# Gathered rows of a mixture-of-experts block, turned by VectorE in 32x32 squares instead of by TensorE

## The reference, cut to what matters

```python
def expert_block(args):                    # xb: 128 rows (tokens) of one expert
    xb, e = args
    gu = xb @ w_gate_up[e] + b_gate_up[e]  # 1024 -> 2048
    gate, up = gu[:, :D_EXPERT], gu[:, D_EXPERT:]
    gate = jnp.minimum(gate, SWIGLU_LIMIT)
    up = jnp.clip(up, -SWIGLU_LIMIT, SWIGLU_LIMIT)
    act = (up + 1) * (gate * jax.nn.sigmoid(SWIGLU_ALPHA * gate))
    return act @ w_down[e] + b_down[e]     # 1024 -> 1024
xs = hp[row_tok].reshape(n_blocks, MOE_BLOCK, D)      # rows gathered by expert
ys = lax.map(expert_block, (xs, block_e)).reshape(p_max, D)
```

## Time and profile before

| | |
|---|---|
| median of 3 runs | 1661.62 us (1660.86 to 1662.49) |
| span of the profiled execution (first to last instruction) | 1658.6 us |
| the profiled execution's own time beyond its span | not given; the median lies 3.0 us above the span |
| PE busy | 1623.4 us, 98% |
| DVE busy | 1349.3 us, 81% |
| ACT busy | 1096.4 us, 66% |
| POOL busy | 303.9 us, 18% |

### The profile page before, as it was taken

The page is one execution under the profiler, slowest core; times in us unless marked ns, Lnnn a source line. Parts: engine busy times, 40 slices in busy tenths (PEclk is TensorE's granted clock), DMA queues, the critical chain, the costliest instruction groups (busy, mean ns, idle before and its releaser), DMA issues.

```text
span 1658.6 us, 24749 instructions
## 1 busy us (share of the span) xinstructions
PE 1623.4 (98%) x8080; PEld 1342.5 (81%) x8080; DVE 1349.3 (81%) x1098; ACT 1096.4 (66%) x1002; POOL 303.9 (18%) x204
## 2 busy tenths in 40 slices
PE   8999999999989999999999999999999999999995
PEld 6797777788887888888888888888888888888884
DVE  6974555423668999999999999999999999999994
ACT  5433444322356777877877778878778878778873
POOL 0000000401006622412211112111112111122110
PEclk8999999999998999999999999999999999999998
DMA  8331222432449999999999999999999999999993
GB/s 249 107 102 51 77 77 77 130 102 87 162 174 352 335 368 390 385 387 371 366 384 385 387 374 370 377 388 387 385 368 365 387 386 385 387 371 362 390 386 87
DMA packets 115018, 483.42 MB, mean 291 GB/s; under 512 B 13371, under 2 KB 56599, under 8 KB 65687
## 3 DMA queue, kind: packets, MB, share of 16 engines
q1 hardware_dynamic: 103892, 454.43, 70.0%
q0 software_dynamic: 11088, 28.48, 8.0%
HBM read 469.51 MB, written 22.26 MB: 297 GB/s over the span
## 4 chain that ended last, share of the span: by engine, by line
PE 92%; DVE 3%; POOL 1%; issue 1%; ACT 1%; DMA 1%; SPq 0%; ACTq 0%; DVEq 0%; POOLq 0%
PE ps L621 29%; PE ps L623 28%; PE ps L622 28%; PE ps L849 2%; PE ps L843 2%; DVE work L1402 2%; POOL slot_records L1709 1%; PE ps L730 1%; PE ps L750 1%; PE ps L739 1%; PE ps L879 1%; PE ps L885 0%; DMA r<-in_x 0%; DVE r L1410 0%; ACT zT L976 0%
## 5 line engine op out<-in xcount | busy, mean ns | idle before, releaser
L1278 DVE TENSOR_TENSOR zT<-raw,zT 128x2048 fp32r<-128x2048 f32 x96 | 217.8, 2294 | 48.8 <-ACT zT L976 48.8
L1278 DVE TENSOR_TENSOR zT<-more_raw,zT 128x2048 fp32r<-128x2048 f32 x96 | 220.2, 2294 | 12.7 <-ACT zT L976 12.6
L1278 DVE TENSOR_TENSOR w_lo<-raw,w_hi 128x2048 fp32r<-128x2048 f32 x96 | 219.0, 2286 | 4.7 <-ACT w_hi L976 1.7
L976 ACT ACTIVATE w_hi<-raw 128x2048 fp32r<-128x2048 f32 x96 | 184.2, 1918 | 53.2 <-PE ps L623 53.2
L1278 DVE TENSOR_TENSOR w_lo<-more_raw,w_hi 128x2048 fp32r<-128x2048 f32 x96 | 217.7, 2294 | 1.3 <-ACT w_hi L976 0.4
L621 PE MATMUL ps<-zT,xT 128*128 128x512 f32 x512 | 203.0, 396 | 0.5 <-DVE zT L1278 0.5
L976 ACT ACTIVATE zT<-more_raw 128x2048 fp32r<-128x2048 f32 x96 | 183.5, 1912 | 27.0 <-PE ps L623 27.0
L621 PE MATMUL ps<-w_hi,xT 128*128 128x512 f32 x512 | 199.8, 390 | 1.5 <-DVE xT L1534 1.0
L623 PE MATMUL ps<-zT,xT 128*128 128x512 f32 x512 | 199.8, 390 | 0.0
L622 PE MATMUL ps<-zT,xT 128*128 128x512 f32 x512 | 199.7, 390 | 0.0
L623 PE MATMUL ps<-w_hi,xT 128*128 128x512 f32 x512 | 199.6, 390 | 0.0
(11 more groups left out here) (265 smaller groups left out, 3288.2 us busy)
## 6 DMA issues: line engine op xcount, KB each, us to landing
more_raw<-in_w_gate_up SPq DMA_DIRECT2D x129, 1024.0 KB, 7.7
raw<-in_w_gate_up SPq DMA_DIRECT2D x127, 1024.0 KB, 8.5
raw<-in_w_down SPq DMA_DIRECT2D x65, 1024.0 KB, 8.2
more_raw<-in_w_down SPq DMA_DIRECT2D x63, 1024.0 KB, 7.7
raw<-in_w_in SPq DMA_DIRECT2D x29, 1024.0 KB, 5.4
r<-in_x SPq DMA_DIRECT2D x8, 512.0 KB, 6.2
raw<-in_w_branch_conv SPq DMA_DIRECT2D x4, 1024.0 KB, 5.4
raw<-in_w_out SPq DMA_DIRECT2D x4, 1024.0 KB, 5.0
```

The lines of the kernel that those rows point to most:

```text
L976: nc.scalar.activation(expert_pair(0, c), chunk, ACT.Copy).then_inc(split_hi, 2)
L1278: nc.vector.tensor_tensor(expert_pair(1, c), chunk, expert_pair(0, c).bitcast(F32), ALU.subtract).then_inc(split_lo, 2)
```

## The change

The 128 rows of a block are gathered as four quarters for each token: four indirect DMAs of 128 pieces of 1 KB instead of one of 128 rows of 4 KB. The 32 partitions of group b receive quarter b of the features, so that squares of 32x32 are all that is left to turn. One VectorE instruction turns the whole 128x1024 block square by square into a plain SBUF buffer `rows_raw` (`turn_rows`, in DVE's order behind split 10). ACT makes `xTh` from that buffer in one instruction (`rows`), DVE makes `xTl` in one (`rest_of_rows`). PE's transposes of rows are gone except those of block 0, which go into `aTh` and `aTl` (the activations' buffers, free then). The quarter row numbers of blocks 1 and 2 need one more small matmul; those of later blocks come from four more reads of the records and one GpSimd operation ahead of the first scatter.

```diff
@@ PE
-    if j == 10:
-        next_rows(0, 0)
-next_rows(0, 1)
 with pe.Fori(1, nblk) as g:
-    pe.wait_ge(turned_read, tile(g, BEGIN) - 1)
+    pe.wait_ge(rows_lo, g)
...
     for k in range(KD):
         down(g, 16 + k, k)
-        if k == 3:
-            next_rows(g, 0)
-            next_rows(g, 1)
@@ PE, ahead of block 0
+pe.wait_ge(early_parts, 2)
+pe.matmul(ps[:, 1, 2 * P:2 * P + NQ * (EARLY - 1)], cst[:, C_SAME:C_SAME + P], by_part[:, :], start=True,
+          stop=True).then_inc(early_quarters, 1)
@@ ACT
+def rows(g, units, later):
+    if units is not None:
+        sc.wait_ge(used, units)
+    sc.wait_ge(rows_turned, later)
+    nc.scalar.activation(xTh, rows_raw.rearrange("p (k n) -> p k n", n=P), ACT.Copy).then_inc(rows_hi, 1)
...
-    turned(g, ROWS0, xTh[:, 0:4, :], bk_T)
-    turned(g, ROWS1, xTh[:, 4:8, :], bk_T + 1)
+    rows(g, unit_base(g) + 16, g + 1)
@@ DVE
+def turn_rows(g):
+    ve.wait_ge(xs_in, 16 + 16 * NQ * g)
+    if not isinstance(g, int) or g > 1:
+        ve.wait_ge(rows_lo, g - 1)
+    nc.vector.transpose(rows_raw.rearrange("p (k b j) -> p k b j", k=KD, b=NQ),
+                        quarters.rearrange("p b (i k) -> p k b i", k=KD)).then_inc(rows_turned, 1)
+def rest_of_rows(g):
+    ve.wait_ge(rows_hi, g)
+    nc.vector.tensor_tensor(xTl, rows_raw.rearrange("p (k n) -> p k n", n=P), xTh.bitcast(F32),
+                            ALU.subtract).then_inc(rows_lo, 1)
...
+    if c == 10:
+        turn_rows(g + 1)
     if c in (10, 11):
         gate_part(g, c - 10)
         up_part(g, c - 10)
-turned(g, ROWS0, xTh[:, 0:4, :], xTl[:, 0:4, :], bk_T)
-turned(g, ROWS1, xTh[:, 4:8, :], xTl[:, 4:8, :], bk_T + 1)
+rest_of_rows(g + 1)
@@ POOL
-def gather(col=0):
-    nc.gpsimd.indirect_dma_start(
-        out=xs, out_offset=None, in_=h2_dram,
+def gather_quarters(kept):
+    for part in range(NQ):
+        nc.gpsimd.indirect_dma_start(
+            out=quarters[:, part, :], out_offset=None, in_=h2_quarters,
...
+for part in range(NQ):
+    gp.dma_start(quarter_slots[PQ * part:PQ * part + PQ], slot_dram.rearrange(
+        "(b j c) i -> j b c i", b=NQ, j=PQ)).then_inc(slots_in, 16)
...
-gp.wait_ge(slots_in, 16)
+gp.wait_ge(slots_in, 16 * (1 + NQ))
+nc.gpsimd.tensor_scalar(quarter_rows.rearrange("p c b -> p b c"), quarter_slots[:, :, :, 0], float(NQ),
+                        cst[:, C_QUARTER:C_QUARTER + 1], ALU.mult, ALU.add).then_inc(quarter_rows_ok, 1)
+gp.wait_ge(quarter_rows_ok, 1)
```

More of the change, by code:

```diff
@@ L63 @@
 NREC = NB * TOPK
-C_END = C_REC + NREC
+NQ = 4
+C_PART = C_REC + NREC
+C_QUARTER = C_PART + NQ
+C_SAME = C_QUARTER + 1
+C_END = C_SAME + P
+QW = D // NQ
+PQ = P // NQ
 FILL = 11
@@ L401, in hybrid_block, with tile, hi_tile @@
         rows_free = sem("rows_free")
-        BEGIN, ACT0, ACT1, ROWS0, ROWS1 = range(5)
         FIRST_ROWS = 3
[L410 to L415, removed]
+        def tile(g, half):
+            return 2 * g + (2 + half)
+        def hi_tile(g, half):
+            return 2 * g + (1 + half)
         def unit_base(g):
@@ L859, in _, with gate_up @@
             nblk = pe.value_load(ublk[0:1, NCOL:NCOL + 1], min_val=NE, max_val=MAXBLK)
-            def gate_up(g, j, gate_bank=bk_A):
+            def gate_up(g, j, gate_bank=bk_A, hi=xTh, lo=xTl):
                 k, s = divmod(j, 2)
@@ L867, in gate_up @@
                     c = slice(512 * half, 512 * half + 512)
-                    last = three(ps[:, (gate_bank, bk_B)[s] + half, :], xTh[:, k, :], xTl[:, k, :], wh[:, c], wl[:, c],
+                    last = three(ps[:, (gate_bank, bk_B)[s] + half, :], hi[:, k, :], lo[:, k, :], wh[:, c], wl[:, c],
                                  k == 0, k == KD - 1)
@@ L1177, in _ @@
             split_expert(1, 0)
-            turned(0, ROWS0, xTh[:, 0:4, :], bk_T)
+            rows(0, None, 1)
             split_expert(1, 1)
@@ L1585, in _ @@
                 split_expert(0, c)
+                if c == 5:
+                    turn_rows(1)
             split_expert(1, 0)
-            turned(0, ROWS0, xTh[:, 0:4, :], xTl[:, 0:4, :], bk_T)
+            rest_of_rows(1)
             split_expert(1, 1)
@@ L1591, in _ @@
             first_act(0)
-            turned(0, ROWS1, xTh[:, 4:8, :], xTl[:, 4:8, :], bk_T + 1)
             first_act(1)
@@ L1676, in _ @@
             gp.wait_ge(turned_pe, FIRST_ROWS)
-            gp.wait_ge(early_ok, 1)
-            gather(3)
+            gp.wait_ge(early_quarters_ok, 1)
+            gather_quarters(0)
             def place_records():
@@ L1706, in _ @@
                 if n == RECORDS_FIRST:
-                    gp.wait_ge(turned_pe, tile(1, BEGIN))
-                    gather(4)
+                    gp.wait_ge(rows_turned, 1)
+                    gather_quarters(1)
                 nc.gpsimd.indirect_dma_start(
@@ L1751, in gather_next @@
             def gather_next(g):
-                gp.wait_ge(turned_pe, tile(g, BEGIN))
-                nc.gpsimd.tensor_copy(uix[:, 0:1], slots[:, bass.ds(g + 3, 1), 0]).then_inc(column_ok, 1)
+                gp.wait_ge(rows_turned, g)
+                nc.gpsimd.tensor_copy(quarter_at[:, EARLY - 1, :], quarter_rows[:, bass.ds(g + 1, 1), :].rearrange(
+                    "p o b -> p (o b)")).then_inc(column_ok, 1)
                 gp.wait_ge(column_ok, g)
                 gp.sem_inc(gp_step, 1)
-                gather()
+                gather_quarters(EARLY - 1)
             def scatter(g, earlier, outputs):
```

99 lines of the change are left out of this document (60 added, 39 removed).

## The result

The changed kernel takes 1739.99 us (median of 5 runs, 1731.42 to 1741.46) against 1661.95 (5 runs, 1660.86 to 1662.49): the ratio is 1.0462, 95% interval 1.0446 to 1.0477. It is 4.6% slower. 1694 us and a range up to 1732 had been forecast: the direction was right, the size less than half of what came.

A forecast was written before the change was run, and what follows sets the result against it. Bound: a loop through PE's block start and DVE's chain, slack 0.30 us. 30 x 0.76 = 22.8 plus 9.0 at the start gave +31.8, span 1690.4, with 3.0 to the median 1693.4, stated as 1694 us; range 1678 to 1732.

The forecast's parts named there:

- the second loop: PE's block start, 23.04 us to split 10, DVE's 11.83, then 0.1: 34.97 against PE's 35.27, slack 0.30 us.
- The turn comes ... I take the plain subtraction's step, 1.13: On DVE behind split 10: the 128x1024 turn, absent from the trace, priced at 1.13 us per block.
- The bounds (0.65 to 6.6): Limits in us for the turn on DVE: a 1024-element row less overlap below, the slow reciprocal above.
- The turn takes another time than 1.1 to 1.3 us: Sign that the prediction is wrong, read from the turn's row on DVE; 1.2 us was expected.
- The rival of the slow turn: Reads with a 32-byte step make DVE's turn 2.2 us, period 37.1, time 1726 us; chance 0.22.
- had PE wait 1.7 us: PE's wait at each block's start: new loop period 36.03 us less PE's own 34.37.
- two periods of 0.76: Steady part: each period 0.76 us longer, counted 30 times for 22.8 us.
- the chain: DVE without idle time from split 10 to the next block's split 0: 11.83 us, forecast to grow by 1.06.
- Rows removed from PE gain nothing: Eight transposes a block leave PE, 0.90 us, but nothing is left of it since DVE's loop sets the period.
- ACT's copy and the steady gathers are covered: Steady part: ACT's single copy and POOL's four gathers, the latter with 2.9 us of cover, priced at nothing.
- POOL's start, +9.0 us (7 to 13): Start of the expert part: added gathers 5.6, record reads 2.4 and one operation 1.0 us lengthen POOL's chain.
- not faster, for the turn must find its place outside the chain: Rival that PE remains the bound, 1643.6 us, needing DVE's chain to shrink by 0.6 us; chance 0.10.

The follow-up runs named there:

- e1: Changed kernel with ten turns and copies of various steps and widths behind VectorE's last split, which nothing waits for; 1739.34 us, one run.
- e5: Changed kernel plus nine matmuls of 512 columns on PE at each block's start, ahead of its waits; 1726.35 us, ratio 1.0384.
- e2: Changed kernel with the turn reading 32 neighbouring values instead of every eighth, feature order left unmatched to the weights; 1697.86 us, ratio 1.022.
- e6: Changed kernel with VectorE's two activation products moved behind split 1 of the next block, slow turn kept; 1703.14 us, ratio 1.0257.
- e13: e2 with VectorE starting block 1's turn only after GpSimd's fifteen small operations on record positions; 1697.06 us.
- e12: Changed kernel: neighbouring-value turn reads with matching feature order, gathers ahead of scatter, turn behind c = 3, activation products behind next block's split 1; 1653.59 us, ratio 0.9951.
- e7: Kernel before plus two VectorE subtractions, 128x2048 ahead of the first gate part and 128x1024 ahead of the second; 1782.23 us, one run.
- e9: Changed kernel, slow turn kept; from block 3 gathers ahead of scatter, turn behind c = 3, activation products behind next block's split 1; 1762.31 us, ratio 1.0604.
- e3: Changed kernel with a turn of only 128x128 packed values in place of 128x1024; 1669.41 us, ratio 1.0049.
- e4: Kernel before plus one unused 128x1024 subtraction on VectorE ahead of the first gate part; 1691.25 us, ratio 1.0178.

## Why the prediction was wrong in size

**What bounds the kernel, the second loop: right.** Six kernels lie on it. Its constant was 23.25, not 23.14 us, 0.11 x 28 = 3.1 us.

**"The turn comes ... I take the plain subtraction's step, 1.13": the step that failed.** It measured 2.09, 0.96 more in each of 28 periods, 26.9 us of the 38.8 by which the profiled span passed the forecast 1690.4. The bounds (0.65 to 6.6) held it. The choice within them argued that the turn moves one element after another, and that PE reads the same step without loss. The first is what e1 confirms for packed reads (1.245 us); the second was a row of another engine, and it was taken as evidence for DVE. "The turn takes another time than 1.1 to 1.3 us" is also the sign of being wrong that the prediction named. The rival of the slow turn, 2.2 us and a period of 37.1, is what happened; its price of 1726 lacked the clock.

**A term was missing: PE's clock after a wait.** The forecast had PE wait 1.7 us and priced the wait as idle time alone. At 2.33 us the wait costs again: 9 x 1.43 = 12.9 us in the profile, 13.6 us between medians with e5. With the 1.48 us of e2 it would have been nothing, so this term hangs on the first. The turn, the constant and the clock make 42.9 us; the start, forecast at 9.0 and two periods of 0.76, came 3.0 short (7.5 us to block 3), and the other steps of the chain 0.03 us a block. That gives 39.1 us for the 38.8.

**Rows removed from PE gain nothing, ACT's copy and the steady gathers are covered: right**, in the changed kernel: PE waits at block starts alone, and the turn there never waits for its DMA. e6 shows how thin the last cover was.

**POOL's start, +9.0 us (7 to 13): near, but it moves.** The copy came at 576.43 instead of 570.13, +6.3, just under the range, ACT's wait for it was 7.63 us and not about 12, and block 3 started 7.5 later. In e1, whose code is the same up to the last block, these starts were +10.5 (580.60) and +12.3 (618.17). The span of e1 is 7.9 us longer than that of the first profile; 4.8 of it is this start, which may be part of what the other runs of the changed kernel took beyond 1731; those have no profile. The forecast counted the instructions added. What moves the start by 5 us from run to run is not shown: GpSimd's small operations beside DVE's splits made `record_at` 6.7 us later in e1, but in e13, where they were short, the copy came no earlier (583.33 against 582.48 in e2), for the reads landed later.

**The chances.** 0.86 for slower was right, and so was "not faster, for the turn must find its place outside the chain": e12 is that case, and it needed four edits more.

## What to carry to other kernels

Look for the loop, not the busy share: here an engine with 2 us of idle time in each block held the period, and each us put between the head of its wait and the next block's start was paid 28 times. Price an operation that the trace lacks by rows of its own engine and its own step in memory, and time it alone before use; let reads within a row of 32 values lie side by side. Once an engine is made gapless, see what GpSimd has to do beside it, and keep PE's waits short or fill them.

## What was not expected of the hardware

- TensorE, in full work at 2.4 GHz, ran some 3 us of its next work at 1.2 GHz with 9 of 28 waits of 2.3 us, every third. The granted clock fell also with 14 of 28 waits of 2.8 us (e7) and with all 17 of 3.5 us (e9); with none of the waits at block starts of 0.5, 0.6 and 1.5 us (e3, e4, e2), but once with one of 1.56 us (e12). Nine idle matmuls in the wait of 2.3 us removed it (e5).
- A 32x32 turn on VectorE: 1.04 ns a value a partition at steps of 4 and 8 bytes, 1.75 at 16, 1.83 to 1.85 at 32.
- A GpSimd operation of 0.2 us took up to 15.24 us, and the issue of a scatter 7.9 to 8.6 instead of 1.87 to 2.98 (e6), beside VectorE's subtractions with both inputs in SBUF; beside the turn 0.22. At the start of e1 three such operations took 2.2 us each, the length of one split; why the 15.24 us outlasted seven is open.
- A load of the same bytes from a source with four outer rows had a busy share of 0.25 of the 16 DMA engines, 93 GB/s, and the steady part came at 130 GB/s instead of 355.
